# Feed-forward matmuls with 256 columns each, or with their columns taken from both halves of a row in turn

## The reference

```python
# first block
h = rms_norm(x, ffn_norm_g[l])
gate_pre, val = jnp.split(h @ w_up[l], 2, axis=-1)        # 1024 -> 2 * 2816
gate_c = causal_dwconv(gate_pre, conv_w[l], conv_b[l])
x = x + (jax.nn.silu(gate_c) * val) @ w_down[l]           # 2816 -> 1024
...
# each of two layers of the second block
h = rmsnorm(x, ffn_norm_g[l])
g = jnp.einsum("bsd,df->bsf", h, w_gate)
u = jnp.einsum("bsd,df->bsf", h, w_up)
x = x + jnp.einsum("bsf,fd->bsd", jax.nn.silu(g) * u, w_down)
```

## Time and profile before

| what | us |
|---|---|
| two executions | 1885.12 and 1886.47, median 1885.8 |
| span of the profiled execution, first to last instruction | 1883.6 |
| what lies around that span, against the median | 2.2 |
| TensorE matmul busy in the span | 1856.2 (99%) |
| TensorE weight load busy | 1495.2 (79%) |
| GpSimd busy | 1105.9 (59%) |
| VectorE busy | 848.3 (45%) |
| ScalarE busy | 729.8 (39%) |

### The profile page before, as it was taken

One profiled execution on the slowest core, in us unless ns is written; L12 is line 12 of the kernel. 1 busy time (PEld: TensorE's weight loads), 2 busy tenths in 40 slices (PEclk: granted clock), 3 DMA queues, 4 the chain that ended last, 5 costly groups with the idle time before them and its releaser, 6 DMA issues.

```text
span 1883.6 us, 28786 instructions
## 1 busy us (share of the span) xinstructions
PE 1856.2 (99%) x8588; PEld 1495.2 (79%) x8588; DVE 848.3 (45%) x1374; ACT 729.8 (39%) x1159; POOL 1105.9 (59%) x1310
## 2 busy tenths in 40 slices
PE   8999999999999999999999999999999999999998
PEld 6776678888888888867888888888867888888886
DVE  7777643455555112776533333111776533333112
ACT  5245552432322232476432332223476433332222
POOL 5442236567676665875556556566775555655663
PEclk9999999999999999999999999999999999999999
DMA  7211112322222333321232332332322232232332
GB/s 254 76 59 46 57 49 98 100 89 101 94 95 100 101 109 103 113 74 61 90 100 90 100 100 90 103 109 101 113 72 73 80 100 96 94 100 95 103 104 78
DMA packets 52405, 177.47 MB, mean 94 GB/s; under 512 B 6832, under 2 KB 8112, under 8 KB 52080
## 3 DMA queue, kind: packets, MB, share of 16 engines
q1 hardware_dynamic: 52336, 176.57, 28.6%
HBM read 168.84 MB, written 2.10 MB: 91 GB/s over the span
## 4 chain that ended last, share of the span: by engine, by line
PE 91%; DVE 5%; ACT 2%; DVEq 1%; issue 1%; DMA 0%; SPq 0%; ACTq 0%
PE bank L572 23%; PE bank L552 23%; PE bank L553 23%; PE bank L609 3%; PE bank L610 3%; PE bank L616 3%; PE bank L800 1%; PE bank L847 1%; PE bank L833 1%; PE bank L592 1%; PE bank L586 1%; PE bank L587 1%; PE bank L648 1%; PE bank L641 1%; PE bank L640 1%; PE bank L661 1%
## 5 line engine op out<-in xcount | busy, mean ns | idle before, releaser
L497 POOL TENSOR_TENSOR wl<-raw,wh (+1 forms) x1244 | 1020.0, 851 | 734.9 <-ACT wh L1045 734.2
L1045 ACT ACTIVATE wh<-raw 128x1024 fp32r (+1 forms) x311 | 329.7, 1060 | 822.0 <-PE bank L572 683.6
L552 PE MATMUL bank<-xh,wh 128*128 128x512 f32 x1336 | 523.3, 392 | 0.0
L553 PE MATMUL bank<-xl,wh 128*128 128x512 f32 x1336 | 520.3, 389 | 0.0
L572 PE MATMUL bank<-xh,wl 128*128 128x512 f32 x1336 | 338.7, 392 | 0.0
L552 PEld LDWEIGHTS bank<-xh,wh 128*128 128x128 f32 x1336 | 251.2, 188 | 53.1 <-ACT lv L1045 0.7
L553 PEld LDWEIGHTS bank<-xl,wh 128*128 128x128 f32 x1336 | 250.9, 188 | 51.6
L572 PEld LDWEIGHTS bank<-xh,wl 128*128 128x128 f32 x1336 | 248.2, 188 | 52.5 <-issue 2.5
L552 PE MATMUL bank<-hh,wh 128*128 128x512 f32 x528 | 205.4, 389 | 0.0
L553 PE MATMUL bank<-hl,wh 128*128 128x512 f32 x528 | 205.4, 389 | 0.0
L1490 DVE TENSOR_TENSOR ybuf<-bank,rstd 128x512 f32<-128x512 f32 x95 | 65.4, 689 | 239.5 <-PE bank L572 237.5
(11 more groups left out here) (300 smaller groups left out, 2175.6 us busy)
## 6 DMA issues: line engine op xcount, KB each, us to landing
raw<-in_weights SPq DMA_DIRECT2D x311, 512.0 KB, 3.4
turned<-ybuf SPq DMA_DIRECT2D x64, 64.0 KB, 2.0
xs<-in_x SPq DMA_DIRECT2D x4, 512.0 KB, 6.6
out_t<-xs SPq DMA_DIRECT2D x8, 256.0 KB, 2.0
w1k<-in_w SPq DMA_DIRECT2D x1, 1024.0 KB, 9.9
w1v<-in_w SPq DMA_DIRECT2D x1, 1024.0 KB, 11.2
shifted<-kvraw SPq DMA_DIRECT2D x8, 124.0 KB, 2.3
posi<-in_positions SPq DMA_DIRECT2D x2, 256.0 KB, 9.1
```

The source lines that it names most:

```text
L497: x_ = pool.tensor_tensor(wl[:, :, :].rearrange("p s n -> p (s n)")[:, two], raw[:, cols((v % 4) * (CB * P) + h * part, part)], wh[:, :, : ...
L552: mm(b[:, :], w, kh(k), start=first and k == 0, stop=False)
L553: mm(b[:, :], w, kl(k), start=False, stop=False)
L1045: return act.activation(o, i, ACT.Copy, scale=scale)
```

## The change

`out_and_ffn`, `xk`, `tile` and `down` get an argument `order`. Where it is given, `tile` hands over to the new function `ordered`, which issues the same products in the same sequence with the same waits, but passes each through `streams`:

- `order == "halves"`: two matmuls of 256 columns in place of one of 512, the first half of the tokens and then the second. Each of them has its own weight load.
- `order == g`, a number: still one matmul of 512 columns, but both the columns that it reads in SBUF and those that it writes in PSUM are taken in the sequence 0..g-1, 256..256+g-1, g..2g-1, 256+g..256+2g-1, and so on: g neighbouring columns of the first half, then g of the second.

| stage | order | matmuls before | matmuls now |
|---|---|---|---|
| first block, up projection (34 of 44 tiles) | 4 | 816 | 816 |
| first block, down projection | halves | 528 | 1056 |
| first layer, up projection (34 of 44 tiles) | 16 | 816 | 816 |
| first layer, down projection | 2 | 528 | 528 |
| second layer, up projection | none, as before | 816 | 816 |
| second layer, down projection | 32 | 528 | 528 |

```diff
             def tile(t, n, kh, kl, blocks=CB, blk0=0, first=True, last=True, count=True, feed=None, mid=None,
-                     slots=None, feed_sem=None, lag=1, bank_=None):
-
+                     slots=None, feed_sem=None, lag=1, bank_=None, order=None):
+
+                if order is not None:
+                    return ordered(t, n, kh, kl, blocks, blk0, first, last, lag, bank_, order)
...
+            def streams(o, i, order):
+
+                if order == "halves":
+                    return [(o[:, c:c + S // 2], i[:, c:c + S // 2]) for c in (0, S // 2)]
+                a, b = (x_.rearrange("p (h c g) -> p c h g", h=2, g=order) for x_ in (o, i))
+                return [(a, b)]
+
+            def ordered(t, n, kh, kl, blocks, blk0, first, last, lag, bank_, order):
+
+                s, b = t.even(), G[n.even()] if bank_ is None else bank_
+                if first:
+                    wait(pe, tile_out, n + -lag)
+                pe.wait_ge(hi_ready, (t + 1).value())
+                for k in range(blocks):
+                    w = wh[:, s, (blk0 + k) * P:(blk0 + k + 1) * P]
+                    for j, src in enumerate((kh(k), kl(k))):
+                        for c, (o, i) in enumerate(streams(b[:, :], src, order)):
+                            mm(o, w, i, start=first and k == 0 and j == 0 and c == 0, stop=False,
+                               skip_group_check=True)
+                pe.wait_ge(lo_ready, (t + 1).value())
+                for k in range(blocks):
+                    for o, i in streams(b[:, :], kh(k), order):
+                        x_ = mm(o, wl[:, s, (blk0 + k) * P:(blk0 + k + 1) * P], i, start=False,
+                                stop=last and k == blocks - 1, skip_group_check=True)
+                x_.then_inc(chunk_done, 1)
...
-                        xk((tb + m).loop(r, 2), (nb + m).loop(r, 2))
+                        xk((tb + m).loop(r, 2), (nb + m).loop(r, 2), order=order)
...
-                                 blocks=min(CB, KF - k0), first=c == 0, last=c == DOWN_CHUNKS - 1)
+                                 blocks=min(CB, KF - k0), first=c == 0, last=c == DOWN_CHUNKS - 1, order=order)
...
             tb, nb = out_and_ffn(Count(T_IN + T_MIX), Count(N_IN + N_MIX), (mh, ml), (R["mix_lo"], Count(0)),
-                                 Count(8), Count(KD))
-            down(tb, nb, Count(KF))
+                                 Count(8), Count(KD), 4)
+            down(tb, nb, Count(KF), "halves")
...
-                                     Count(3 * KD).loop(l, 2 * KD))
-                down(tb, nb, Count(2 * KF).loop(l, KF))
+                                     Count(3 * KD).loop(l, 2 * KD), (16, None)[l])
+                down(tb, nb, Count(2 * KF).loop(l, KF), (2, 32)[l])
```

More of the change, by code:

```diff
@@ L623, in xgroup, with xk @@
                 group(t, lambda k: xh[:, k, :], lambda k: xl[:, k, :], feed, xl_ready, hooks)
-            def xk(t, n, feed=None, mid=None, slots=None, lag=1, bank_=None):
+            def xk(t, n, feed=None, mid=None, slots=None, lag=1, bank_=None, order=None):
                 tile(t, n, lambda k: xh[:, k, :], lambda k: xl[:, k, :], feed=feed, mid=mid, slots=slots, lag=lag,
-                     bank_=bank_)
+                     bank_=bank_, order=order)
             def vgroup(t, n, hooks):
@@ L884, in _, with out_and_ffn @@
                          count=m == 1)
-            def out_and_ffn(tb, nb, ysrc, y_ready, u, feed):
+            def out_and_ffn(tb, nb, ysrc, y_ready, u, feed, order):
                 group(tb, lambda k: ysrc[0][:, k, :], lambda k: ysrc[1][:, k, :], y_ready[1], y_ready[0], {})
@@ L900, in out_and_ffn, with down @@
                     for m in range(10, 12):
-                        xk((tb + m).loop(r, 2), (nb + m).loop(r, 2))
+                        xk((tb + m).loop(r, 2), (nb + m).loop(r, 2), order=order)
                 tb, nb = tb + T_UP, nb + T_UP
                 return tb, nb
-            def down(tb, nb, h_lo):
+            def down(tb, nb, h_lo, order):
                 with pe.Fori(0, KD // 2) as r:
```

## The result

The changed kernel takes 1981.45 us (two executions, 1981.41 and 1981.50), 1.0508 of the kernel before, 95% interval 1.0491 to 1.0526. It is 95.7 us slower, where 9.8 us had been forecast.

The account below looks back on a forecast made before the run. The prediction took TensorE's matmul pace, with no cover, to bound the kernel. Terms of 7.0 + 0 + 2.8 = 9.8 us, added to the 1883.6 us span and 2.2 us to the median, gave 1896 us; range 1876 to 2010.

Parts of the forecast that it names:

- What bounds the kernel: In the five changed loop stages TensorE is always busy, so the price is matmul count times change of pace, without cover.
- Part 1: First block's down projection in 256-column halves: 1056 matmuls at 120 ns, 126.7 us against 119.7, so +7.0 us.
- 13.3 ns a matmul: Time left beyond estimated column streaming in the 226.7 ns of an F32R matmul, assumed to stay with each 256-column matmul.
- rival D: First block's down projection: halves bound by the 188 ns weight load, +78.8 us, 1965 us in all; chance 0.05.
- Part 2: Groups of 4, 16 and 32 columns, 2160 matmuls: no change from 226.7 ns; bounds -28.5 and +432 us.
- Part 3: First layer's down projection, groups of 2, 528 matmuls: 232 ns each, +2.8 us; bounds -7.0 and +105.8 us.
- wandering pace of rows 10: Trace before the change, after a phase with short matmuls: nine matmuls in 2.09 us, 232 ns each instead of 226.7.
- Part of the 13 ns looks like two streams getting in each other's way: F32R matmuls: some of the leftover beyond streaming was read as matmul stream and weight load disturbing each other; could be larger.
- A: Jumping columns in PSUM cost like broken-up writes, 200 ns a matmul for groups of 2: +214 us, 2107 us; chance 0.12.
- B: Stages with groups: each jump costs one column's time, 0.417 ns, +114 us, 2007 us in all; chance 0.08.
- C: Only groups of 2, first layer's down projection, pay, at plain float32 pace: +105.8 us, 1999 us in all; chance 0.06.
- E: Changed stages: alternating takes the two streams out of each other's way, -35.5 us, 1848 us in all; chance 0.07.

## Why the prediction was right or wrong

- **What bounds the kernel: right.** TensorE's pace times the number of matmuls, with no cover. The stages add up to 95.7 us of 95.65.
- **Part 1, halves: right.** 120.0 ns each and +7.0 us, to the digit. The 13.3 ns a matmul behind it held at three widths with full loads. That it held is in part luck: with loads of 64 columns the same matmul of 256 had 6.6 ns left over and not 13.3, and what the 13.3 ns are made of is not known. Of the widths measured, full loads bound a matmul only at 128 columns: 111.6 ns measured, 111 read from the earlier trace rows, which also disposes of rival D.
- **Part 2, groups of 4, 16 and 32: wrong.** The failed step is "The nearest row is the same matmul with its normal row, 226.7 ns, and I take no change". They cost 23.3, 13.3 and 10.0 ns, 35.2 us in all, and all of it comes from the reads. The nearest row was no evidence, because equal columns and bytes do not make equal reads: the same 128 whole pieces took between 223.4 and 278.1 ns by their order alone. The term was put at nothing without a reason. For groups of 4 the two surcharges above fit; why groups of 8, 16 and 32 cost what they do stays open.
- **Part 3, groups of 2: wrong.** That the finest groups would cost the most was right. The failed step is "I take the wandering pace of rows 10, 232 ns, because that is what the trace shows when the two streams disturb each other": those rows have straight reads, and nothing in them measured a jump. It took 328.0 ns, +53.5 us instead of +2.8, 56% of the whole difference. With loads of half the size it took 331.1, so it is no clash with the weight load either. The plain float32 pace of 427 ns held as an upper bound here, but it is none for reads in general: half pieces in sequence took 453.3.
- **"Part of the 13 ns looks like two streams getting in each other's way": half refuted.** 10.8 of the 13.3 ns went when the same piece was read again and again, with the load running all the same. Smaller loads took nothing away at 512 and 384 columns, and half of it at 256.
- **Rivals.** A is refuted where it was put: PSUM writes cost nothing. B, one column's time a jump, said 107, 53, 13 and 7 ns; measured 101, 23, 13 and 10, and its 2007 us lay on the right side, but groups of 64 (3 ns by it) cost nothing, and repeated or skipping orders with as many jumps are free, so it is no rule. C had the right stage as the largest, at twice its price and with nothing for the others. D, 1965 us, and C, 1999, lie nearest to 1981, by chance: neither has the mechanism. E, that alternating helps, was refuted for this change; that some order of columns is faster than the straight one turned out true for every fourth piece.
- **Chances.** Slower by over 2% had 0.31, and the range up to 2010 held the result. That it did is luck, since it was drawn to take in B, C and D, none of which holds. Its lower end, 1876, is said to be where the forecast's own gain side ends, which a few lines earlier is 1880. The likeliest case should have been weighed less: the pipe was known to be full, and an unseen access pattern was counted as free.

## What to carry to other kernels

With F32R matmuls at full pace the order in which the moving operand is read shows at once in the time. It should be read in whole aligned 16-byte pieces and in long runs (64 columns were enough here). Jumping to the other half of the row after every two columns cost 45%, jumping after groups of 4 that lie across two pieces 47%, and half pieces in sequence 100%. PSUM could be written in every order tested here, down to aligned pairs, for free, so a permutation that helps the reads can simply be followed on the write side. Where the trace shows an engine full and has no row for a new access pattern, measure that pattern in one stage before it goes into five, and let the six stages of one kernel be six measurements.

## What the runs showed of the hardware that had not been expected

- Writes to PSUM that jump by half a bank after every two float32 values: 226.7 ns, as straight ones.
- Two passes of half pieces take 453.3 ns, twice the 226.7 of 512 straight columns, and a repeated piece 215.8 ns: the sequence of pieces read sets the pace as much as the number of columns.
- The order of whole pieces alone moves a matmul between 223.4 and 278.1 ns; every fourth piece is faster than a straight row.
- A smaller weight load can make a matmul slower: 230.0 ns with 64 weight columns (and so 64 output rows) against 226.7 with 128.
